# 64 instead of 32 tokens outside the dense products of a PEER layer, with low parts shared between two engines

## What is computed

```
def block(args):
    hx, idx, w = args
    ue = jnp.take(u, idx, axis=0)
    act = jnp.einsum('td,tkd->tk', hx, ue).astype(jnp.float32)
    coef = (w * jax.nn.gelu(act, approximate=False)).astype(h.dtype)
    ve = jnp.take(v, idx, axis=0)
    return jnp.einsum('tk,tkd->td', coef, ve)
```

## Time and profile before

| | us |
|---|---|
| device time, median of 3 runs | 1468.03 |
| lowest and highest | 1467.85, 1470.13 |
| the profiled execution's own time | 1469.01 |
| its span, first to last instruction | 1467.2 |
| PE busy | 1441.1 (98%) |
| DVE busy | 1223.1 (83%) |
| ACT busy | 579.9 (40%) |
| POOL busy | 643.7 (44%) |
| DMA, mean over the span | 294 GB/s |

### The profile page before, as it was taken

One profiled execution on the slowest core, in us unless ns is written; L12 is line 12 of the kernel. 1 busy time (PEld: TensorE's weight loads), 2 busy tenths in 40 slices (PEclk: granted clock), 3 DMA queues, 4 the chain that ended last, 5 costly groups with the idle time before them and its releaser, 6 DMA issues.

```text
span 1467.2 us, 22340 instructions
## 1 busy us (share of the span) xinstructions
PE 1441.1 (98%) x8191; PEld 1270.7 (87%) x8191; DVE 1223.1 (83%) x2510; ACT 579.9 (40%) x877; POOL 643.7 (44%) x461
## 2 busy tenths in 40 slices
...
GB/s 377 296 259 98 135 98 115 43 101 158 125 223 321 328 316 283 279 373 394 389 378 378 285 345 362 351 385 415 348 370 365 377 367 372 358 379 373 368 352 137
DMA packets 164777, 432.00 MB, mean 294 GB/s; under 512 B 18656, under 2 KB 67552, under 8 KB 164704
## 3 DMA queue, kind: packets, MB, share of 16 engines
...
...
HBM read 385.70 MB, written 45.37 MB: 294 GB/s over the span
## 4 chain that ended last, share of the span: by engine, by line
PE 79%; DVE 16%; DMA 2%; ACT 1%; issue 1%; POOL 0%; SPq 0%; ACTq 0%; DVEq 0%
PE ps L1908 24%; PE ps L1909 24%; PE ps L1910 24%; PE ps L2316 3%; DVE rows L1664 2%; DVE ps L1698 1%; DVE ps L1702 1%; DVE picks L1704 1%; DMA ada_w<-w_ada 1%; PE ps L2254 1%; DMA g_dram<-g_buf 1%; DVE tv L1622 1%; DVE tv L1625 1%; DVE cand L1675 1%; DVE ti L1623 1%
## 5 line engine op out<-in xcount | busy, mean ns | idle before, releaser
L1908 PE MATMUL ps<-hT_hi,ws_hi 128*128 128x352 f32 (+1 forms) x992 | 336.5, 339 | 2.3 <-ACT g_buf L1065 1.1
L1909 PE MATMUL ps<-hT_lo,ws_hi 128*128 128x352 f32 (+1 forms) x992 | 331.1, 334 | 0.0
L1910 PE MATMUL ps<-hT_hi,ws_lo 128*128 128x352 f32 (+1 forms) x992 | 330.8, 334 | 0.0
L1908 PE MATMUL ps<-vs_hi,coef_hi 128*128 128x512 f32 x768 | 299.0, 389 | 1.2 <-DVE coef_lo L1865 1.2
L1909 PE MATMUL ps<-vs_lo,coef_hi 128*128 128x512 f32 x768 | 298.8, 389 | 0.0
L1910 PE MATMUL ps<-vs_hi,coef_lo 128*128 128x512 f32 x768 | 298.8, 389 | 0.0
L1106 ACT ACTIVATE vs_hi<-blk_raw 128x1024 fp32r<-128x1024 f32 x128 | 135.6, 1060 | 244.4 <-PE ps L1910 241.4
L749 POOL DMA_INDIRECT rows<-u_nat,ids x128 | 151.6, 1184 | 181.2 <-DVE sp_act L1664 158.6
L772 POOL TENSOR_TENSOR vs_lo<-blk_raw,vs_hi 128x1024 fp32r<-128x1024 f32 x60 | 144.1, 2401 | 144.4 <-DVE coef_lo L1865 144.4
L1050 ACT ACTIVATE ws_hi<-blk_raw 128x1024 fp32r<-128x1024 f32 x104 | 110.1, 1059 | 219.4 <-PE ps L1910 219.0
L1908 PEld LDWEIGHTS ps<-hT_hi,ws_hi 128*128 128x128 f32 x992 | 186.8, 188 | 9.7 <-issue 4.1
...
## 6 DMA issues: line engine op xcount, KB each, us to landing
blk_raw<-u_t SPq DMA_DIRECT2D x128, 512.0 KB, 5.8
blk_raw<-v_nat SPq DMA_DIRECT2D x128, 512.0 KB, 6.9
...
w_dram<-w_stage SPq DMA_DIRECT2D x32, 512.0 KB, 10.9
grp_w<-w_dram ACTq DMA_DIRECT2D x31, 512.0 KB, 13.9
part_w<-w_ada POOLq DMA_DIRECT2D x24, 512.0 KB, 6.3
raw<-w_in SPq DMA_DIRECT2D x20, 512.0 KB, 6.6
```

The costliest lines, as they stand in the source:

```text
L1908: pe.matmul(o, lh, rh, start=start, stop=False, skip_group_check=True)
L1909: pe.matmul(o, lh, rl, start=False, stop=False, skip_group_check=True)
L1910: return pe.matmul(o, ll, rh, start=False, stop=stop, skip_group_check=True)
```

## The change

FEW becomes 64: the products have 320 columns, g_dram holds 320 columns a block, and 64 row operations instead of 32 serve the few tokens, two groups of 64. Their gelu goes no longer through HBM: ACT writes it onto the blocks of a diagonal (`few_diag`), and one matmul with a folded identity (`few_eye`) turns it. Eight one-hot steps instead of four have three terms, and they stand apart, behind blocks 115 to 122. PART_A is 52. From block 55 on POOL makes the low part of every odd block, as soon as DVE has the one-hots of the block two ahead, and DVE that of the even ones; odd blocks use slot 1 and a new slot in the unused last 128 columns of hT_hi and hT_lo in turn. Rows stand behind odd blocks only: two, or three where there is no step. 63 U rows instead of 26 move into the V stage, its first 42 blocks, and the V rows into blocks 44 to 123. The kept weights are loaded at block 123 instead of 114. PE's blocks from 52 on are written out instead of looped.

```diff
-FEW = 32
+FEW = 64
...
-PART_A = 48
+PART_A = 52
...
-PART_END = PART_A + STEPS // 7 * 8 + STEPS % 7
+PART_END = PART_A + FEW_STEP // 7 * 8 + FEW_STEP % 7
+FEW_AT = 115
...
+    if FEW_AT <= b < FEW_AT + STEPS - FEW_STEP:
+        return FEW_STEP + b - FEW_AT
...
-FEW_GELU, FEW_TURN, FEW_COEF = PART_A + 34, PART_A + 38, PART_A + 47
-RES_W_AT = EB - 14
-V_ACT = 26
-V_ACT_END = 20
+FEW_GELU, FEW_TURN, FEW_COEF = FEW_AT - 4, FEW_AT - 2, FEW_AT - 1
+RES_W_AT = EB - 5
+V_ACT = 63
+V_ACT_END = 42
...
+    if b % 2 == 0:
+        return 0
+    if b < PART_END:
+        return 3 if spreads_after(b) is None else 2
+    if spreads_after(b) is not None:
+        return 2
+    early = sum(act_rows(i) for i in range(PART_A, PART_END)) + STEPS - FEW_STEP
+    places = [i for i in range(PART_END | 1, EB, 2) if spreads_after(i) is None]
+    return share(U_ROWS - V_ACT - FIRST_ROWS - early, places.index(b), len(places))
...
+def u_by_pool(b):
+
+    return b % 2 == 1 and REST_DVE <= b < EB - U_RING
...
-            return b % WS_U if b < PART_A else b % 2
+            if b < PART_A:
+                return b % WS_U
+            return (0, 1, 0, WS_U)[b % 4]
+
+        def us(parts, b_slot):
+
+            if b_slot == WS_U:
+                return (hT_hi if parts is us_hi else hT_lo)[:, :, ND:N]
+            return parts[b_slot][:].rearrange("p (c n) -> p c n", c=KC)
...
-                if FEW_TURN <= b < FEW_TURN + FEW_G:
-                    g = b - FEW_TURN
-                    sp.wait_ge(few_moved, 16 * (FEW_G + 1))
-                    sp.dma_start(few_coef[g * FEW_J:(g + 1) * FEW_J, 0, :],
...
+                    if b % 2 and u_by_pool(b + 2):
+                        if b < PART_END or spreads_after(b) is not None:
+                            pool.wait_ge(oh_done, max(q for q in map(spreads_after, (b - 1, b)) if q is not None) + 1)
+                        else:
+                            pool.wait_ge(*rest_of_u(b - 1))
+                        rest(b + 2)
...
-                    act.activation(kept[:, NU:ND], ones[:, 0:FEW], ACT.Copy)
-                    act.activation(kept[:, 0:NU], ps[:, b % 2, 0:NU], ACT.Gelu).then_inc(gelu_done, 1)
+                    act.activation(kept[:], ps[:, b % 2, 0:NU], ACT.Gelu).then_inc(gelu_done, 1)
...
-                elif PART_A <= b and b + 2 < EB:
+                elif PART_A <= b and b % 2 == 0 and b + 2 < EB:
                     round_u(b + 2, act_done, b + 1)
                 gelu(b)
...
+                if PART_A <= b and b % 2 == 0 and b + 3 < EB:
+                    round_u(b + 3, act_done, b + 1)
...
-                if b >= REST_DVE:
+                if b >= REST_DVE and not u_by_pool(b):
                     rest_u(b)
...
+                e = expert_block(v)
+                dve.tensor_copy(coef[:, v % 2, NU:ND], w_stage[:, 1, e, :])
+                dve.tensor_tensor(coef[:, v % 2, SENT_COLS:NU], values[:, SENT_COLS:NU], w_stage[:, 0, e, :], ALU.mult)
...
+                if b == FEW_TURN:
+                    pe.wait_ge(iotas, 21)
+                    pe.wait_ge(sp_gelu, 1)
+                    pe.matmul(ps[:, 4, 0:FEW], few_diag[:], few_eye[:], start=True, stop=True).then_inc(ptr_done, 1)
+                products(b % 2, u_slot(b), b - 1, *rest_of_u(b))
```

More of the change, by code:

```diff
@@ L773, in rest_v @@
                                    ALU.subtract).then_inc(u_lo, 1)
-            k, read = sum(len(due) for due in placed), U_ROWS - V_ACT
-            for b in range(-1, EB):
-                if b >= 0:
-                    if pool_rest(b):
-                        rest_v(b)
-                    read += v_rows(b)
+            k, read = sum(len(due) for due in placed), FIRST_ROWS
+            for b in range(PART_A, 2 * EB):
+                if b < EB:
+                    if b % 2 and u_by_pool(b + 2):
[4 more added lines that the diff above has]
+                        rest(b + 2)
+                    read += act_rows(b)
+                else:
+                    if pool_rest(b - EB):
+                        rest_v(b - EB)
+                    read += v_rows(b - EB)
                 while k < U_ROWS + PICKS and row_behind(k) < read:
@@ L1049, in round_u @@
                 act.wait_ge(used, used_value)
[L1050 removed]
+                act.activation(us(us_hi, u_slot(b)), raw_u(b), ACT.Copy).then_inc(u_hi, 1)
             def gelu(b):
@@ L2292, in _, with products @@
             key_scores(2 * PH - 1)
-            def products(b, p, w, free):
-                pe.wait_ge(u_lo, b + 1)
+            def products(p, w, free, low, low_done):
+                pe.wait_ge(low, low_done)
                 if free is not None:
                     pe.wait_ge(gelu_done, free)
-                hi = us_hi[w][:].rearrange("p (c n) -> p c n", c=KC)
-                lo = us_lo[w][:].rearrange("p (c n) -> p c n", c=KC)
+                hi, lo = us(us_hi, w), us(us_lo, w)
                 for kc in range(KC):
@@ L2330, in _ @@
                 last.then_inc(ptr_done, 1)
-            products(PART_A - 1, 1, WS_U - 1, PART_A - 2)
+            products(1, WS_U - 1, PART_A - 2, u_lo, PART_A)
             def few_columns():
```

112 lines of the change are left out of this document (52 added, 60 removed).

## The result

| | before | after |
|---|---|---|
| device time, median (us) | 1468.98 | 1485.22 |
| lowest and highest | 1467.85, 1470.13 | 1480.37, 1490.01 |
| the profiled execution's own time | 1469.01 | 1486.25 |
| its span | 1467.2 | 1484.4 |
| PE busy | 1441.1 (98%) | 1416.2 (95%) |

The ratio is 1.0111, with a 95% interval of 1.0085 to 1.0138: the changed kernel is slower, by 1.1%, where 1430.5 was forecast and 1424 to 1446 was the range. (The kernel before has one execution more here than in the table ahead of the prediction.)

The account below looks back on a forecast made before the run. PE's matmul stream, plus one 7.98 us wait for DVE's softmax weights, was taken as the bound. Terms of -15.4, -24.6, -1.5, +1.8, +0.5, +1.0, -1.1 and +1.3 summed to -38.0 from 1469.0: forecast 1430.5 us, range 1424 to 1446.

Parts of the forecast that it names:

- DVE and GpSimd beside the one-hot blocks: U blocks with one-hots: DVE needs 8.4 us a pair against PE's 8.96, POOL's low part has time to spare; 0.
- 320 columns: U stage matmuls shortened from 352 columns: 0.32 us less in each of 77 blocks behind the transposes, -24.6 us.
- four blocks ahead: PART_A from 48 to 52: four more U blocks done ahead of the transposes in the same time, -15.4 us.
- The rival by which weight loads take over: U stage: below 352 columns weight loading sets the pace, so 24.6 us are missing and time is 1455; 4%.
- Ahead of the transposes: End of the searches: POOL's delays stay hidden, one shorter wait and an early row gathered sooner gain 0 to 3, taken -1.5.
- a cover of 9: PE's wait ahead of the transposes, some 9 us, inside which PE's losses to POOL and gathers were to cost 0.
- The kept weights' load: Load moved to block 123 behind the last store, -1.1 us; perhaps 2 or 3 late, costing nothing more at V's start.
- Store stops in blocks 97 to 114: 18 U blocks without one-hots: late stores stop gelu and then PE, +1.0 us (0 to 4).
- The V stage: V matmuls unchanged and DVE's lead lasts, 0; a third row in the first pair delays the start, +1.3 us.
- V falls behind: Rival in the V stage: gathers land later, DVE waits and its lead is used up; 1434 to 1444 us; 20%.
- a ceiling of 370 GB/s: Rival: DMA queues sustain no more than the V stage's earlier mean of 370 GB/s, making transfers the bound; 4%.
- Slower than before: Rival in late U blocks and V stage: transfers are the bound, V blocks take 4.48 us, time 1482; 4%.

Follow-up runs that it names:

- run 8: Run 5 plus DVE's copy of the softmax weights moved behind its copies out of PSUM, with PART_A 48 instead of 52: 1453.77 us.
- run 1: The changed kernel with DVE making every low part of U, none on POOL: 1453.85 us.
- run 2: The changed kernel with ACT rounding the odd block's high part one block earlier: 1448.28 us.
- Runs 3 and 4: The kernel before with 37 unused POOL operations on 128x1024 tiles added: subtractions 1509.20 us, memsets instead 1469.31 us.
- run 9: Run 5 plus DVE's softmax-weights copy moved later, POOL writing zeros instead of low parts for blocks 0 to 51 (not usable): 1423.77 us.
- run 5: Run 2 with the load of the kept weights issued behind block 121 instead of 123: 1443.95 us.
- Run 11: Run 5 plus DVE's softmax-weights copy moved later, with 71 instead of 63 U rows in the V stage: 1445.89 us.

## Why the prediction was wrong, point by point

The step that failed is the term of 0 for DVE and GpSimd beside the one-hot blocks. It is the second point below.

- **320 columns** (-24.6) and **four blocks ahead** (-15.4): right. 146.7 ns a matmul; 3.52 and 4.48 us a block wherever PE doesn't wait; run 8 prices the second at 14.8. The rival by which weight loads take over fell. By the rule of the Trainium skill on LDWEIGHTS ("Perfetto Trace Analysis", Identifying the Most-Contended Engine) there was no headroom; loads that looked busy 98% of the time left room for shorter matmuls.
- **"DVE and GpSimd beside the one-hot blocks ... 0"**: the step that failed. It sized POOL's low part at 2.4 us, allowed that "a DVE operation on two SBUF tiles holds it up", and looked at this one direction only, not at what the subtraction does to DVE. DVE's pair is not 8.4 us but 8.4 + 1.8 = 10.2, against PE's 8.96. It made +24.4 between blocks 53 and 97, +10 of the 14.0 between 97 and 115 and +4.7 between 115 and 123: 39 us, of which run 1 gives back 31 in these stretches and run 2 38. Runs 3 and 4 show it alone. The trace of before held the hint: one comparison in the searches took 4.56 us, three took 2.30. It held the other half as well: in its V stage POOL makes 60 subtractions, nearly all beside rows, which read PSUM, and only one DVE operation is lengthened (a product of 0.29 us that took 2.49).
- **Ahead of the transposes** (-1.5): wrong, +5.4. The forecast had PE lose about 3 us by POOL's pace and 5 together with the gathers that wait for a row buffer, inside a cover of 9. Its 3.80 us a block was a mean with interruptions in it: undisturbed, POOL's gathers lie 3.55 apart (535.60 to 539.15), and PE's first 46 blocks took 165.2 us for 161.9, so the 3 were about right. The 2 left for the gathers were not. DVE lost 7.0 us more in held operations than before, and the row behind its last but one search began at 552.96 instead of 545.63. A gather waited 8.36 us for the buffer of that row, the low part of block 47 stood behind it, and PE stopped for 8.52. The timeline of POOL:

```profile
554.47 2.75 POOL L780 DMA_INDIRECT rows<-u_nat,ids  x1 [8.36 <-DVE sp_act L1709]
```

  and of PE:

```profile
559.65 0.64 PE L1954 MATMUL ps<-hT_hi,us_hi 128*128 128x320 f32 x1 [8.52 <-POOL us_lo L765]
...
578.01 1.15 PE L2374 MATMUL ps<-ident,picks 128*128 128x128 f32 x9
...
589.76 1.37 PE L2361 MATMUL ps<-onehot 128*128 128x128 f16 x16 [3.29 <-DVE onehot L1821]
```

  The cover was used up: the transposes stand right behind block 50, without a wait, and DVE's weights had been there for half a us. So both engines were late, by the same operations of DVE; run 9 takes both delays away together and doesn't price them apart. Behind the transposes the held copy and one more held operation (2.44 us for 0.96) come ahead of PE's wait of 3.29 for the first one-hots.
- **The kept weights' load, "costs nothing more"** (-1.1): wrong, by 4.8 us. "2 or 3 late" was 5.8, and the wait fell on the V stage's first block, not on the second, which waits anyway (run 5).
- **Store stops in blocks 97 to 114** (+1.0): too small by some 4. Rows that come late are part of it:

```profile
822.20 1.22 DVE L1709 CUSTOM_DVE_ANT_0 rows<-rows,ps 128x1024 f32<-128x1024 f32 x1 [3.15 <-DMA rows<-u_nat,few_row_ids]
...
824.06 1.22 DVE L1709 CUSTOM_DVE_ANT_0 rows<-rows,ps 128x1024 f32<-128x1024 f32 x1 [0.63 <-DMA rows<-u_nat,few_row_ids]
...
827.11 1.22 DVE L1709 CUSTOM_DVE_ANT_0 rows<-rows,ps 128x1024 f32<-128x1024 f32 x1 [1.82 <-DMA rows<-u_nat,few_row_ids]
...
828.26 2.99 DVE L1866 TENSOR_TENSOR ws_lo<-blk_raw,ws_hi 128x1024 fp32r<-128x1024 f32 x1
```

  Three rows came 3.15, 0.63 and 1.82 us late, and then a subtraction held the low part behind them. Run 11 shows that fewer rows hardly help; what sets these delays stays open.
- **The V stage** (0, +1.3 at its start): right. Blocks of 4.08, a lead of DVE of 8.8 to 9.9 from block 17 to block 125, 524.7 us in all. The 20% for "V falls behind" and the 4% for a ceiling of 370 GB/s were both against a stage that held:

```profile
DMA packets 52838, 160.64 MB, mean 402 GB/s; under 512 B 4808, under 2 KB 17603, under 8 KB 52827
...
rows<-v_nat,ids POOLq DMA_INDIRECT x111, 7.6
```

  The figure of the Trainium skill ("DMA: Bandwidth & Descriptors", Specifications) of about 358 GB/s a core was no bound here: 402 were held for 400 us. The same page explains under "Bandwidth" that a core gets this share when both cores of an HBM domain stream, and this kernel runs on one core, so the prediction read it too strictly. But run 11 shows that rival's mechanism, a lead used up by late gathers, 8 rows further on.
- **"Slower than before"** came true at 1485, near the 1482 of that rival, by another cause. A number that agrees proves no mechanism.
- **The sum** slips by half a us: 1431.0 less 1.0 is 1430.0, not 1430.5. Nothing hangs on it.
